# A causal mask moved from TensorE to VectorE, and a new order at the first pair of MLP blocks, in a two-layer hybrid decoder

## The reference, cut to what matters

```
def causal_block_attention(q, k, v, scale):
...
        sc = jnp.einsum('bqhd,bkhd->bhqk', qi, k).astype(jnp.float32) * scale
        qpos = i * Q_BLOCK + jnp.arange(Q_BLOCK)
        mask = kpos[None, :] <= qpos[:, None]
        sc = jnp.where(mask[None, None], sc, -jnp.inf)
        p = jax.nn.softmax(sc, axis=-1).astype(v.dtype)
        return jnp.einsum('bhqk,bkhd->bqhd', p, v)
...
        hm = rms_norm(x, mlp_norm_g[l]) @ w_mlp1[l]
        x = x + jnp.square(jax.nn.relu(hm)) @ w_mlp2[l]
```

## Time and profile before

| | |
|---|---|
| median of 3 runs | 2910.28 us (2908.45 to 2910.64) |
| the profiled execution's own time | 2910.69 us |
| its span | 2908.5 us |
| granted TensorE clock over the span | 0.997 |
| layer 0's sweep | 197.3 to 403.4 us |
| layer 1's sweep | 1635.2 to 1844.2 us |

### The profile page before, as it was taken

One profiled execution on the slowest core, in us unless ns is written; L12 is line 12 of the kernel. 1 busy time (PEld: TensorE's weight loads), 2 busy tenths in 40 slices (PEclk: granted clock), 3 DMA queues, 4 the chain that ended last, 5 costly groups with the idle time before them and its releaser, 6 DMA issues.

```text
span 2908.5 us, 36837 instructions
## 1 busy us (share of the span) xinstructions
PE 2853.2 (98%) x13294; PEld 2224.0 (76%) x13294; DVE 1535.9 (53%) x1949; ACT 859.6 (30%) x1436; POOL 1560.2 (54%) x1157
## 2 busy tenths in 40 slices
PE   8999999999999999999999999999999999999998
PEld 6766668886878888888887666688878788888886
DVE  8585556024565445554685755650346555545555
ACT  3455553223321111110214655432324111101113
POOL 4333343441487777777644224334315877777776
PEclk9999999999999999999999999999999999999999
DMA  3100011220111111111111000113101111111112
GB/s 135 48 10 5 16 37 51 87 87 15 44 44 58 47 43 54 58 50 42 64 58 34 14 1 16 45 50 109 59 22 43 40 54 58 50 43 51 58 53 78
DMA packets 61423, 140.37 MB, mean 48 GB/s; under 512 B 9232, under 2 KB 11280, under 8 KB 60688
## 3 DMA queue, kind: packets, MB, share of 16 engines
q1 hardware_dynamic: 61328, 139.06, 14.3%
HBM read 134.58 MB, written 4.46 MB: 48 GB/s over the span
## 4 chain that ended last, share of the span: by engine, by line
PE 84%; DVE 6%; POOL 4%; ACT 2%; issue 2%; DMA 1%; SPq 0%; POOLq 0%; DVEq 0%; ACTq 0%
PE ps L1351 22%; PE ps L1335 19%; PE ps L839 16%; PE ps L1207 6%; PE ps L1061 4%; PE ps L1091 2%; PE ps L1263 2%; PE ps L1287 2%; PE ps L1077 2%; PE ps L1222 1%; PE ps L955 1%; PE ps L1238 1%; DVE xbc L1842 1%; PE ps L1157 1%; POOL hT L743 1%
## 5 line engine op out<-in xcount | busy, mean ns | idle before, releaser
L1351 PE MATMUL ps<-hm_h,ring 128*128 128x512 f32 x2048 | 641.3, 391 | 6.9 <-DVE hm_l L2161 4.8
L2169 DVE TENSOR_TENSOR x<-ps,x 128x512 f32<-128x512 f32 x512 | 351.7, 689 | 272.1 <-PE ps L1351 271.5
L748 POOL TENSOR_TENSOR ring<-raw,ones 128x512 fp32r<-128x512 f32 x338 | 354.9, 1050 | 260.3 <-PE ps L1351 202.3
L1351 PEld LDWEIGHTS ps<-hm_h,ring 128*128 128x128 f32 x2048 | 384.4, 188 | 101.3 <-issue 17.0
L751 POOL TENSOR_TENSOR ring<-raw,ring 128x512 fp32r<-128x512 f32 x338 | 439.4, 1300 | 26.4
L839 PE MATMUL ps<-hA,wsp 128*128 128x512 f32 x1920 | 443.2, 392 | 1.6 <-POOL wsp L603 1.1
L600 POOL TENSOR_TENSOR wsp<-raw,ones 128x1024 fp32r<-128x1024 f32 x63 | 124.6, 1978 | 565.9 <-PE ps L839 453.1
L839 PEld LDWEIGHTS ps<-hA,wsp 128*128 128x128 f32 x1920 | 360.3, 188 | 82.6 <-issue 6.7
L1351 PE MATMUL ps<-hm_l,ring 128*128 128x512 f32 x1024 | 398.6, 389 | 0.0
L1335 PE MATMUL ps<-hT,ring 128*128 128x512 f32 x1440 | 332.0, 389 | 1.5 <-POOL ring L751 1.5
L1335 PEld LDWEIGHTS ps<-hT,ring 128*128 128x128 f32 x1440 | 270.1, 188 | 58.6 <-POOL ring L751 2.3
(11 more groups left out here) (306 smaller groups left out, 3935.6 us busy)
## 6 DMA issues: line engine op xcount, KB each, us to landing
raw<-in_weight_tiles SPq DMA_DIRECT2D x248, 256.0 KB, 2.6
raw<-in_weight_tiles SPq DMA_DIRECT2D x108, 512.0 KB, 3.3
outT<-x SPq DMA_DIRECT2D x16, 256.0 KB, 2.2
x<-in_xT SPq DMA_DIRECT2D x3, 1024.0 KB, 10.2
wh<-in_head_weights SPq DMA_DIRECT2D x8, 256.0 KB, 2.7
raw_early<-in_weight_tiles SPq DMA_DIRECT2D x4, 512.0 KB, 3.7
mem_s<-in_memT SPq DMA_DIRECT2D x2, 1024.0 KB, 4.8
x<-in_xT SPq DMA_DIRECT2D x2, 512.0 KB, 5.2
```

The lines of the kernel that those rows point to most:

```text
L748: pool.tensor_tensor(ring[:, slot, 0, :], blk(i), ones[:, 0:1].to_broadcast([P, HT]), ALU.mult).then_inc(op_ready[slot], 1)
L1351: last = pe.matmul(ps[:, bank, :], w[:, part, k, (m % 2) * P:(m % 2 + 1) * P], h[k][:, cols_of(half)], start=(k == 0 and part == 0 and h i ...
L2169: dve.tensor_tensor(xm, ps[:, bank, :], xm, ALU.add).then_inc(x_add, 1)
```

## The change

The product with `future` goes from PE, and with it the identity `ident_h` and its two instructions at the start on POOL. DVE adds `future` to the diagonal block in PSUM ahead of the maximum, through `link`. In the MLP's first pair, the high parts of W2 blocks 2 and 3 are made by ACT instead of POOL, behind the fourth hidden tile; ACT finishes that tile before it rounds the last two sums of group 2; DVE does the fourth hidden tile before these two sums, and its subtraction between them.

```diff
@@ pool: constants
-                pool.memset(ident_h[:, :], 0.0)
...
-                pool.affine_select(out=ident_h[:, :], in_=ident_h[:, :], compare_op=ALU.not_equal, fill=1.0,
-                                   base=0, pattern=[[-1, P]], channel_multiplier=1)
@@ pool: first_second(j)
-                        split_op(W2_BLK[j], j, 0)
+                        if j < 2:
+                            split_op(W2_BLK[j], j, 0)
+                        else:
+                            pool.wait_ge(op_ready[j], here(op_ready[j], 1))
+                            pool.tensor_tensor(ring[:, j, 1, :], blk(W2_BLK[j]), ring[:, j, 0, :].bitcast(F32),
+                                               ALU.subtract).then_inc(op_ready[j], 1)
+                            pool.wait_ge(op_ready[j], here(op_ready[j], 2))
@@ tensor: scores(n)
-                            edge = j + 4 > i
                             last = pe.matmul(dst, q[0:DQ, i * P:(i + 1) * P], k[0:DQ, j * P:j * P + w],
-                                             start=True, stop=not edge)
-                            if edge:
-                                last = pe.matmul(ps[:, 2 * (n % 2) + j // 4, w - P:w], ident_h[:, :], future[:, :],
-                                                 start=False, stop=True)
+                                             start=True, stop=True)
@@ scalar: MLP, first pair
+                    hidden_hi(4, 3, 1, 1)
+                    act.wait_ge(t_ready[1], here(t_ready[1], U_MLP + 1))
+                    for j in (2, 3):
+                        act.wait_ge(blk_ready[W2_BLK[j]], here(blk_ready[W2_BLK[j]], 16))
+                        act.activation(ring[:, j, 0, :], blk(W2_BLK[j]), ACT.Copy).then_inc(op_ready[j], 1)
                     high_sums(2, slice(2, 4))
-                    hidden_hi(4, 3, 1, 1)
@@ vector: row_max(n)
                         w = (unit(n)[1] + 1) * P
+                        diagonal = banks(2 * (n % 2))[:, w - P:w]
+                        link(dve.tensor_tensor(diagonal, diagonal, future[:, :], ALU.add))
                         dve.tensor_reduce(stat(nmx, n), banks(2 * (n % 2))[:, 0:w], AX.X, ALU.max, negate=True).then_inc(s_max, 1)
@@ vector: MLP, first pair
-                    sum_of(2, 2)
-                    sum_of(2, 3)
                     dve.wait_ge(t_ready[1], here(t_ready[1], U_MLP + 1))
                     hidden(3, 1)
+                    sum_of(2, 2)
                     hidden_lo(4, 3, 1, 1)
+                    sum_of(2, 3)
```

More of the change, by code:

```diff
@@ L317, in trunk @@
         esum = at("esum", o + 760, [P, 2, NBLK])
-        ident_h = at("ident_h", o + 504, [P, P], BF16)
         future = at("future", CST + 1792, [P, P], BF16)
```

## The result

| | median | lowest to highest |
|---|---|---|
| before | 2910.28 us | 2908.45 to 2910.64 |
| the change | 2924.75 us | 2920.16 to 2926.28 |

The ratio is 1.0045, 95% interval 1.0035 to 1.0056: slower by some 14.5 us. The profiled execution of the change took 2925.72 us with a span of 2923.7 us, 15.2 us more than before. Its granted clock over the span was 0.995; the five executions had 0.995 to 0.998, and the one at 0.998 was the fastest. In two of the kernels further down, fill_short and mlp_fill_short, one of seven executions took 10,261 and 9,220 us: their medians are of all seven (without that one they are 0.3 and 0.1 us lower), and the ranges given leave it out.

A forecast was written before the change was run, and what follows sets the result against it. PE was taken to bound most of the kernel, POOL the MLP's first pair, with softmax chains over DVE and ACT making PE wait in the sweep; 12.3 - 4.8 = +7.5 us on 2910.69 us gave 2918.0 us, range 2911.5 to 2926.

The forecast's parts named there:

- rival 4: DVE fills up in the sweep: 0.39 us an add, 2.2 us from the MLP, 2924.3 us; chance 0.14.
- The price of an addition: Mask add on DVE ahead of each maximum: 0.28 us plus 0.04 us for the wait for its own end.
- Places A to D: Four places per pair of heads where PE waits for softmax chains: together 1.54 us a pair, 12.3 us for eight.
- A: Third row of blocks, outputs at 259.73: two adds on one chain lengthen PE's wait for `probT`, 0.42 us.
- B: Outputs at 271.21, behind the next pair's query rotations: the adds of two units stack, 0.33 us.
- C: Decay product at 281.82, waiting for ACT's `EL`: two adds on the chain ahead, 0.53 us.
- D: End of the pair, outputs at 298.54: one add ahead of the last unit's maximum, no slack, 0.26 us.
- Four equal pairs a layer: Causal sweep: a pair of heads repeats every 52.34 us, four in each of two layers, each losing 1.54 us.
- The product's 0.06 us: Removed mask product, per unit: its PE time gains nothing where PE waits; only 0.06 us of earlier scores counts.
- rival 1: PE decides everywhere, adds fit beside it, removed products count in full (7.7 us): 2897.8 us; chance 0.08.
- The MLP: MLP's first pair, bound by POOL: losing two rounding multiplies of W2 blocks gains 2.39 us a layer, 4.8 us in all.
- Rivals 2 and 3: Cheap add of 0.22 us, no change, 2911.4 us, chance 0.18; MLP's new order gains nothing, 2922.8 us, chance 0.06.

The follow-up runs named there:

- fill_short: mask_only plus 42 short transposes of the identity in TensorE's waits in the fourth pair of heads: 2920.23 us, ratio 1.0029.
- mlp_fill_short: mlp_only plus 28 short transposes of the identity in the fourth pair of heads: 2902.26 us, ratio 0.9970.
- dummy_free: Kernel before, mask product kept, plus a VectorE addition into spare tiles ahead of each maximum, without `link`: 2918.68 us, ratio 1.0025.
- no_mask: Kernel before with neither mask product nor mask addition, so the mask is left out: 2905.98 us, ratio 0.9982.
- dummy_linked: Kernel before, mask product kept, plus a VectorE addition into a spare tile ahead of each maximum, with `link`: 2928.24 us, ratio 1.0057.
- mask_only: Kernel before with only the mask parts of the change, the MLP in its old order: 2927.57 us, ratio 1.0056.
- last_on_dve: Kernel before with the mask addition on VectorE only in each layer's fourth pair of heads, product elsewhere: 2912.43 us, ratio 1.0006.
- mlp_only: Kernel before with only the MLP parts of the change, the mask still on TensorE: 2908.91 us, ratio 0.9990.

## Why the prediction was right, point by point

The median of 2924.75 us lies in the range (2911.5 to 2926) and on the side that had the chance of 0.67, but 6.8 us above the forecast of 2918.0. That it lies in the range is luck: the range reached up to 2926 for rival 4, which did not occur, and a term of 6.0 us that the forecast did not have filled that room.

- **The price of an addition**, 0.28 + 0.04 us: 0.30 + 0.04. Right. The overlap that the wait forbids was taken as 0.06 us; the row cited for it shows 0.09 (240.02 + 0.29 against 240.22) and dummy_free 0.08.
- **Places A to D**: forecast 0.42 + 0.33 + 0.53 + 0.26 = 1.54 us a pair, measured 0.55 + 0.50 + 0.60 - 0.28 + 0.22 = 1.59. The period of "about 53.9 us" came out as 53.93. The sum hid two errors: A, B and C were sized 0.13, 0.17 and 0.07 us too small, D 0.04 too large, and the 0.28 us that come back between C and D were not in it. At A the forecast wait for `probT` of 0.5 us and more did not come (0.21 us); PE waited 0.45 us for `prob` instead, for which the prediction had no term. Why A and B are larger stays open.
- **Four equal pairs a layer**: at full clock (fill_short) 1.2 us for the first, 1.6, 1.6, and 2.2 for the fourth: 6.6 us a sweep against 6.2, so 13.2 us against the 12.3 of the sum. The prediction took the fourth pair for a repeat of the others; it repeats after 48.24 us before, not 52.34.
- **The product's 0.06 us "worth nothing" where PE waits, and rival 1**: no_mask gives 0.80 us of the 0.96 a pair, so the row's 0.06 was right and the rival's rule true of the removal alone. It fell because of what was added; the difference of dummy_linked and mask_only, 0.30 us a pair, is what the removal was worth in the change, near the 4 x 0.06 us that the sum had.
- **The MLP**: forecast 4.8 us, measured 2.3 + 2.1 = 4.4. Right in place and mechanism. POOL saved 2.12 us of the 2.39 in layer 0, because the two subtractions took 0.25 us longer. The 2.3 us is measured against a profile whose stretch of 43.00 us is among the two longest; against the usual 42.6 it is 1.9. The last wait, 1.25 in place of 1.10 us, says nothing: mask_only has 1.25 us there with the old order.
- **What failed is a term that was missing**: the sum let PE's waits cost their own length. In the fourth pair they also lowered the granted clock. Against fill_short's 212.4 us the change's sweeps were 4.4 and 4.5 us longer; less the 2.9 us that before already lost in layer 1, that is 6.0 us. The forecast "sweep some 6 us longer in each layer" was thus 11.0 and 8.2. With 13.2 + 6.0 - 4.4 = 14.8 of the 15.2 us the account closes; the rest is the small stretches of the table. The sign was readable before: the last outputs of layer 1 stood in the trace of before at 5.57 us, against 3.46 everywhere else, and layer 1's sweep took 209.0 us where layer 0's took 206.1 for the same work. The prediction names neither.
- **Rival 4** (2924.3 us) hit the time by another cause: DVE did not fill up, and an add cost 0.34, not 0.39 us. Rivals 2 and 3 fell with the measured add and the measured MLP.

## What to carry to other kernels

Read a repeating piece and its last repetition apart, and compare the same group of instructions across all repetitions: one that took 5.57 us where the others took 3.46 was a clock that had fallen, and here the change, which added waits beside it, paid 6.0 us more than the waits. Moving a cheap operation off the busiest engine onto one that the softmax waits for cost up to the full 0.34 us, the operation and the semaphore behind it, at each of the few places where PE waited for what follows it, while what it freed was 0.06 us; so price the chain that comes behind, not the busy shares. Where waits of TensorE cannot be removed and the clock falls behind them, short transposes that fit inside the wait are worth trying; here products that were longer than the wait gave all of it back.

## What the runs showed of the hardware that I had not expected

- The granted clock fell to 0.50 after waits of PE of 0.6 to 1.8 us each, with work between them, and the same waits left it at 1.00 in last_on_dve and in layer 0 of before. Executions of one kernel spread over 2.2 to 7.3 us, and over 0.6 to 2.8 us where the waits were filled; the five profiles with filled waits have no fall in a sweep.
- Instructions that compute nothing made the kernel faster: with 28 transposes of 0.11 us a layer the median went from 2908.91 us (mlp_only) to 2902.26 (mlp_fill_short), though not all of this is the clock's.
- In float32 a plain product of 128 columns by the identity came as two instructions and 0.23 us, a transpose of the same size as one of 0.11 us.
- A wait between two VectorE operations cost 0.12 us, and 16 of them 1.05 us of a pair's 54.23.
